# Retention heads worked between the units of the gate projection instead of after them

## The reference

```python
proj = h @ w_in                      # queries, keys: 4 heads x 256; values, gate: 4 heads x 512
...                                  # rotate q and k
o = fwd + bwd                        # per head: (q @ k.T * decay) @ v, in both directions
o = o * lax.rsqrt(jnp.mean(o * o, axis=-1, keepdims=True) + RMS_EPS)
return (jax.nn.silu(g) * o) @ w_out  # g: the gate, 2048 wide
```

## Time and profile before

| what | value |
|---|---|
| median of 3 runs | 2352.61 us (2351.33 to 2357.74) |
| the profiled execution, its own time | 2350.38 us |
| its span, first to last instruction | 2348.4 us |
| TensorE, VectorE, ScalarE busy | 98%, 72%, 57% of the span |
| mean granted TensorE clock | 0.999 of full |
| gate units and heads of layer 0 | about 102.4 to 167 us of the span |
| the same of layer 3 | about 1285 to 1349 us |

### The profile page before, as it was taken

The page is one execution under the profiler, slowest core; times in us unless marked ns, Lnnn a source line. Parts: engine busy times, 40 slices in busy tenths (PEclk is TensorE's granted clock), DMA queues, the critical chain, the costliest instruction groups (busy, mean ns, idle before and its releaser), DMA issues.

```text
span 2348.4 us, 55250 instructions
## 1 busy us (share of the span) xinstructions
PE 2309.2 (98%) x19883; PEld 2217.3 (94%) x19883; DVE 1689.1 (72%) x3317; ACT 1343.2 (57%) x2766; POOL 71.5 (3%) x140
## 2 busy tenths in 40 slices
PE   9999999999999999999999999999999999999998
PEld 8899999889998999999998999999898999998998
DVE  7667767977658888776576677658576785677875
ACT  5555556365556556665555565556755554466554
POOL 0000000000001112100000000000000000010000
PEclk9999999999999999999999999999999999999999
DMA  7535665235654455456645446654444555444664
GB/s 246 178 117 170 190 209 174 94 125 162 198 192 136 150 157 158 149 168 196 201 160 178 141 156 188 204 180 147 143 129 130 174 177 179 146 131 142 192 194 145
DMA packets 107520, 387.87 MB, mean 165 GB/s; under 512 B 14432, under 2 KB 16608, under 8 KB 107136
## 3 DMA queue, kind: packets, MB, share of 16 engines
q1 hardware_dynamic: 102656, 380.58, 51.2%
q0 software_dynamic: 4736, 5.58, 0.8%
HBM read 382.93 MB, written 1.05 MB: 164 GB/s over the span
## 4 chain that ended last, share of the span: by engine, by line
PE 83%; DVE 9%; ACT 4%; issue 2%; DMA 1%; POOL 0%; DVEq 0%; ACTq 0%; SPq 0%; POOLq 0%
PE acc L571 24%; PE acc L578 24%; PE acc L577 24%; DVE weights_lo L2178 2%; PE acc L791 1%; PE acc L790 1%; PE acc L789 1%; ACT weights_hi L1336 1%; PE acc L811 1%; DVE h L2337 1%; DVE y L2326 1%; DVE xn_parts L2333 1%; PE acc L724 1%; PE acc L894 1%; PE acc L916 1%
## 5 line engine op out<-in xcount | busy, mean ns | idle before, releaser
L2178 DVE TENSOR_TENSOR weights_lo<-weights,weights_hi 128x512 fp32r<-128x512 f32 (+1 forms) x1160 | 758.6, 680 | 323.6 <-ACT weights_hi L1336 318.9
L1336 ACT ACTIVATE weights_hi<-weights 128x512 fp32r<-128x512 f32 (+1 forms) x1160 | 679.8, 619 | 262.0 <-PE acc L578 233.2
L571 PE MATMUL acc<-xn_parts,weights_hi 128*128 128x256 f32 (+1 forms) x2560 | 726.9, 284 | 9.1 <-DVE weights_lo L2178 6.7
L578 PE MATMUL acc<-xn_parts,weights_lo 128*128 128x256 f32 (+1 forms) x2560 | 716.6, 280 | 0.0
L577 PE MATMUL acc<-xn_parts,weights_hi 128*128 128x256 f32 (+1 forms) x2558 | 716.0, 280 | 0.0
L571 PEld LDWEIGHTS acc<-xn_parts,weights_hi 128*128 128x128 f32 x2560 | 482.0, 188 | 22.9 <-issue 13.2
L571 PE MATMUL acc<-arena_r,weights_hi 128*128 128x256 f32 (+1 forms) x1760 | 494.2, 281 | 3.0 <-DVE weights_lo L2178 1.6
L578 PE MATMUL acc<-arena_r,weights_lo 128*128 128x256 f32 (+1 forms) x1760 | 490.9, 279 | 0.0
L577 PE MATMUL acc<-arena_r,weights_hi 128*128 128x256 f32 (+1 forms) x1754 | 488.8, 279 | 0.0
L578 PEld LDWEIGHTS acc<-xn_parts,weights_lo 128*128 128x128 f32 x2560 | 481.5, 188 | 0.0
L577 PEld LDWEIGHTS acc<-xn_parts,weights_hi 128*128 128x128 f32 x2558 | 481.1, 188 | 0.4
(11 more groups left out here) (341 smaller groups left out, 2302.4 us busy)
## 6 DMA issues: line engine op xcount, KB each, us to landing
weights<-in_ffn_in SPq DMA_DIRECT2D x176, 512.0 KB, 3.9
weights<-in_ffn_out SPq DMA_DIRECT2D x64, 704.0 KB, 4.1
weights<-in_att_in SPq DMA_DIRECT2D x72, 512.0 KB, 3.6
weights<-in_mlp_in SPq DMA_DIRECT2D x64, 512.0 KB, 3.6
weights<-in_mlp_out SPq DMA_DIRECT2D x64, 512.0 KB, 3.6
weights<-in_ret_qk SPq DMA_DIRECT2D x32, 512.0 KB, 4.0
weights<-in_ret_v SPq DMA_DIRECT2D x32, 512.0 KB, 3.9
weights<-in_ret_g SPq DMA_DIRECT2D x32, 512.0 KB, 3.5
```

What stands on the lines that cost most here:

```text
L571: nc.tensor.matmul(acc, hi, src_hi, start=first, stop=False)
L578: return nc.tensor.matmul(acc, lo, src_hi, start=False, stop=last)
L1336: nc.scalar.activation(w_hi[phase.ring(sub)][:, 0:n, :], raw[slot][:, j * SUB:j * SUB + n, :], ACT.Copy)\
L2178: nc.vector.tensor_tensor(w_lo[phase.ring(sub)][:, 0:n, :], raw[slot][:, j * SUB:j * SUB + n, :], w_hi[phase.ring(sub)][:, 0:n, :].bitcast ...
```

## The change

The two functions `ret_gates` and `retention` become one, `gates_and_heads`, on each of the three engines. The 16 gate units run as straight code, without a loop, and the steps of the heads stand between them: after gate unit 4h TensorE takes the mean of the squares of head h-1, weighs head h and computes the scores of head h+2; the other steps stand in fixed places on ScalarE and VectorE. All heads now use banks 6 and 7, so weighing head h waits until "gated" of head h-1 has read them. Banks 2 and 3 take the means, so the gate has two banks instead of four. Head 3 adds its squares on VectorE as the others do (three matmuls fewer). Since silu goes on between the heads, each inverse root is bracketed by two table loads, and the norm of the heads goes to a place of its own (`head_rstd`). After the last gate unit come the eight parts of the output projection. The lines of the kernel after lie some lines off those before.

```diff
+        head_rstd = silu[:, 0, 0:S1]
...
-            def retention(j, layer):
+            def gates_and_heads(j, layer, src):
...
-                def last_mean_square():
...
-                for hd in range(RET_HEADS):
-                    pe.wait_ge(R["p_ready"], 4 * j + hd + 1)
-                    if hd >= 2:
-                        pe.wait_ge(R["gated"], 4 * j + hd - 1)
-                    weigh(hd, 0)
...
+                def gate_unit(n):
+                    pe.wait_ge(out_evacuated, FREE_BANKS + gates.out0 + (n - 1 if n >= 2 else n - 3))
+                    multiply(gates, n // gates.body, n % gates.body, PS[:, n % 2, 0:S1], src, None, n == 3)
+
+                def weigh(hd):
+                    pe.wait_ge(R["p_ready"], 4 * j + hd + 1)
+                    if hd:
+                        pe.wait_ge(R["gated"], 5 * j + hd)
...
+                for n in range(gates.units):
+                    gate_unit(n)
+                    if n % 4 == 0:
+                        hd = n // 4
+                        if hd:
+                            mean_square(hd - 1)
+                        weigh(hd)
+                        if hd + 2 < RET_HEADS:
+                            ret_scores(j, hd + 2)
+                    if n == gates.units - 2:
+                        mean_square(RET_HEADS - 1)
                 part_output(0, 0, 0)
                 part_output(1, 0, 1)
-                last_mean_square()
                 part_output(2, 1, 0, True)
...
+                def inverse_rms(hd):
+                    exp_tables()
+                    act.wait_ge(R["sum_ready"], 4 * j + hd + 1)
+                    step(nc.scalar.activation(lnv[:, 0:S1], PS[:, 2 + hd % 2, 0:S1], ACT.Ln, bias=rms_eps, scale=float(D) / RET_V))
+                    nc.scalar.activation(head_rstd, lnv[:, 0:S1], ACT.Exp, scale=-0.5).then_inc(R["rstd_ready"], 1)
+                    nc.scalar.preload_act_table(ACT.Silu)
...
+                for n in range(gates.units):
+                    hd = n // 4
+                    if n + 1 < gates.units:
+                        split(gates, hd, n % 4 + 1)
+                    else:
+                        split(phase, 0, 0)
+                        inverse_rms(RET_HEADS - 1)
+                    if n % 4 == 1:
+                        if hd:
+                            inverse_rms(hd - 1)
+                        squares_of(hd)
+                    if n % 4 == 2 and hd:
                         rounded(hd - 1)
...
+                    gate(n)
+                split(phase, 0, 1)
+                split_part(phase, 0, 2, 0)
+                rounded(3, 0)
                 split_part(phase, 0, 2, 1)
+                rounded(3, 1)
+                exp_tables()
                 split_part(phase, 0, 3, 0)
...
+                for n in range(gates.units):
+                    hd = n // 4
+                    if n + 1 < gates.units:
+                        split(gates, hd, n % 4 + 1)
+                    else:
+                        split(phase, 0, 0)
+                        gated(3, 0)
+                    if n % 4 == 0 and hd:
+                        gated(hd - 1)
+                    if n % 4 == 1:
+                        if hd:
+                            scale(hd - 1)
                         added(hd)
...
+                    if n % 4 == 2:
+                        if hd:
+                            rest_of_head(hd - 1)
+                        if hd + 2 < RET_HEADS:
+                            decayed(j, hd + 2)
+                    gate(n)
+                split_part(phase, 0, 1, 0)
+                gated(3, 1)
+                split_part(phase, 0, 1, 1)
+                scale(3, 0)
...
```

More of the change, by code:

```diff
@@ L710, in ret_scores @@
                 last.then_inc(ret_sem["scores_ready"], 1)
-            def retention(j, layer):
+            def gates_and_heads(j, layer, src):
                 R = ret_sem
[L716 to L722, removed]
+                gates, phase = ph[f"ret_g{layer}"], ph[f"ret_out{layer}"]
+                def gate_unit(n):
[5 more added lines that the diff above has]
+                        pe.wait_ge(R["gated"], 5 * j + hd)
+                    for e in range(4):
+                        acc = PS[:, 6 + e // 2, (e % 2) * S1:(e % 2 + 1) * S1]
                         for kt in range(2):
@@ L725, in weigh @@
                                                     ret_p[:, hd % 2, kt * S1:(kt + 1) * S1], start=(kt == 0), stop=(kt == 1))
-                    if half:
-                        last.then_inc(R["o_ready"], 1)
+                    last.then_inc(R["o_ready"], 1)
                 def mean_square(hd):
-                    pe.wait_ge(R["squares_added"], 6 * j + 2 * hd + 2)
-                    nc.tensor.matmul(PS[:, hd % 2, 0:S1], mean, ret_sq[:, 0, :], start=True, stop=True).then_inc(R["sum_ready"], 1)
-                def last_mean_square():
[L735 to L738, removed]
+                    pe.wait_ge(R["squares_added"], 8 * j + 2 * hd + 2)
+                    nc.tensor.matmul(PS[:, 2 + hd % 2, 0:S1], mean, ret_sq[:, 0, :], start=True, stop=True).then_inc(R["sum_ready"], 1)
                 def part_output(sub, o, quarter, cut=False):
@@ L2656, in decayed, with gates_and_heads, gate, gated @@
                     .then_inc(ret_sem["p_ready"], 1)
-            def retention(j, layer):
+            def gates_and_heads(j, gates):
                 R = ret_sem
-                phase = ph[f"ret_out{layer}"]
+                phase = gates.after
                 first_split = 5 * j
-                def gated(hd):
-                    first = 6 if hd % 2 == 0 else 2
+                def gate(n):
+                    wait_unit(gates, n // gates.body, n % gates.body)
+                    dve.wait_ge(ret_gate_done, gates.units * j + n + 1)
+                    nc.vector.tensor_tensor(ffn_part[:, n % 4, :], PS[:, n % 2, 0:S1], rstd[:, 0:S1], ALU.mult)\
+                        .then_inc(ret_gate_scaled, 1)
+                    dve.wait_ge(ret_gate_scaled, gates.units * j + n + 1)
+                    dve.sem_inc(out_evacuated, 1)
+                def gated(hd, half=None):
+                    part = slice(0, 4) if half is None else slice(2 * half, 2 * half + 2)
                     dve.wait_ge(R["squares_ready"], 4 * j + hd + 1)
-                    g = proj1[:, 32 + 4 * hd:36 + 4 * hd, :]
-                    nc.vector.tensor_tensor(g, g, PS[:, first:first + 2, :].rearrange("p b (e t) -> p (b e) t", t=S1), ALU.mult)\
+                    dve.wait_ge(ret_gate_done, gates.units * j + 4 + 4 * hd + part.stop)
+                    g = proj1[:, 32 + 4 * hd:36 + 4 * hd, :][:, part, :]
+                    nc.vector.tensor_tensor(g, g, PS[:, 6:8, :].rearrange("p b (e t) -> p (b e) t", t=S1)[:, part, :], ALU.mult)\
                         .then_inc(R["gated"], 1)
@@ L2678, in scale @@
                     part = slice(0, 4) if half is None else slice(2 * half, 2 * half + 2)
-                    dve.wait_ge(R["gated"], 4 * j + hd + 1)
+                    dve.wait_ge(R["gated"], first_split + hd + (half or 0) + 1)
                     dve.wait_ge(R["rstd_ready"], 4 * j + hd + 1)
                     nc.vector.tensor_tensor(ret_o[:, part, :], proj1[:, 32 + 4 * hd:36 + 4 * hd, :][:, part, :],
-                                            spread(rstd[:, 0:S1], part.stop - part.start), ALU.mult).then_inc(R["scaled"], 1)
+                                            spread(head_rstd, part.stop - part.start), ALU.mult).then_inc(R["scaled"], 1)
                 def rest(hd, n):
```

76 lines of the change are left out of this document (15 added, 61 removed).

## The result

The changed kernel takes 2371.64 us (median of 4 runs, 2369.99 to 2374.42), the kernel before 2353.43 on the same chip (2351.33 to 2357.74): 18.2 us more, ratio 1.0077 with a 95% interval of 1.0064 to 1.0089. The forecast was 2369, slower, with a sum of 18.1.

A forecast was written before the change was run, and what follows sets the result against it. TensorE, busy 98% of the span, bounds the kernel. Stalls of 10.65 us plus restarts 0.9 less 2.5 saved make 9.1 a layer, 18.1 for two; added to the profiled 2350.4: 2368.5, forecast 2369, 8-in-10 range 2357 to 2376.

The forecast's parts named there:

- The chain of a gate unit: Scaling, silu, rounding and split on VectorE and ScalarE take 2.63 us against TensorE's 2.83 a unit: 0.2 to spare.
- "gated" before weighing: TensorE waits for VectorE's "gated" before weighing heads 1, 2 and 3: 1.0 us each, 3.0 a layer.
- Units 8, 11 and 12: TensorE waits for VectorE's lo halves at these gate units: 1.6, 0.45 and 1.35 us a layer.
- Output parts: TensorE waits at output projection parts 0, 2 and 6: 1.45, 2.2 and 0.6 us a layer.
- What goes: Two TensorE gaps (0.73 and 0.47) and three matmuls of head 3's mean (1.30) go: 2.5 us a layer.
- The loop that goes: The gate's loop, removed by the change, was said to cost little and was left out of the sum.
- Table loads at 1.30: Each ScalarE table load around a head's inverse root takes 1.30 us, its row in the profile, without a further drain.
- Rival (b): Part of the steps hides, tables costing nothing visible or some stalls overlapping: 2355 to 2362 us; 16%.
- Rival (c): ScalarE's table loads cost twice their row: 2391 us; 4%.
- Rival (a): The heads' steps hide between gate units, since by averages all fits; only 5.0 us go: 2345.4 us; 5%.
- Rival (d): The clock falls at the nine waits, a unit at 1.2 GHz taking 5.65 us: 2420 us; 2%.
- The two signs of an error: Wrong if units 6, 9, 10, 13, 14 were scaled within 0.3 us of their end, or TensorE's steps exceeded 0.118.

The follow-up runs named there:

- all moves: Changed kernel with "gated", "rest" and decay behind scalings, squares before the second table load, head 3's inverse root after the last silu, its last steps later: 2349.87 us.
- the straight gate: Kernel before with only the 16 gate units as straight code in two PSUM banks, heads after them as before: 2349.73 us, ratio 0.9984.
- the changed kernel with cuts: Changed kernel with one matmul of gate units 1, 5, 9 and 13 also cut in two halves, as unit 3 has it: 2373.51 us, ratio 1.0086.

## Why the prediction was right

- **The chain of a gate unit, 2.63 against 2.83.** Right: putting "rest" and the decay behind the scaling takes 9.8 us away without taking work away, and all moves together take 21.8, two table loads a layer among them.
- **"gated" before weighing, 3 x 1.0.** Right in place and releaser and nearly in size: 3.17 + 0.22 for the restarts, against 3.0 + 0.3.
- **Units 8, 11 and 12.** 3.88 + 0.23 against 3.4 + 0.3. Unit 8 waits 0.25 longer than supposed: VectorE has a further 0.18 of idle time before "rest", for ScalarE's rounding of the head (the row at 135.39).
- **Output parts.** 3.95 + 0.32 against 4.25 + 0.3: parts 0 and 2 were put 0.2 and 0.1 too late.
- **What goes, 2.5.** Right: neither the gap at the end of the gate, 0.73, nor that of 0.47 at the output is there after, and three matmuls a layer are gone.
- **The loop that goes, counted as nothing.** Wrong, by little: two turns cost 0.74 in layer 0 and 0.19 in layer 3. With it the terms give 11.77 - 2.51 - 0.74 = 8.5 in layer 0, against 8.6 measured; two small ones cancel (unit 15, which waits 0.1 and restarts, and 0.2 for the restarts behind the two old gaps).
- **The sum of 18.1 against 18.2.** In the two layers the sum is right to 0.5 us: 17.6 were measured. That the whole agrees to 0.1 is luck. The waits were put low, the loop was left out, and the granted clock is in no term: its mean is 0.9973 in the four executions of the changed kernel and 0.9989 in 45 later ones of the kernel before, which is, as an estimate, some 4 us of TensorE's time. What takes as much back elsewhere is not shown. The forecast of 2369 lies below the measured median mostly because the sum was added to the profiled execution, 2350.4, which lies below all four timed ones of its kernel; from their median of 2353.4 it is 2371.5.
- **Table loads at 1.30.** Right: 1.29 in succession. Rival (b) with free loads would be 2360; taking them out gave 2363.3. (In that sum the five stalls named fall by 4.15 and not by 3.9, and two restarts go with them and not three; 4.3 in all stays.) Rival (c), 2391, did not come.
- **Rival (a), the steps hide by averages.** False for this order, and true for another: with all moves they hide.
- **Rival (d), the clock falls at the waits.** Not at the nine waits of the profiled execution, where the clock is 1.00 in both windows above and in the same stretch of layer 3. But it does fall behind waits of this size in others, for less than the rival's price: 1.7 us at a time against 2.8.
- **The two signs of an error.** Units 6, 9, 10, 13 and 14 were scaled 2.3, 1.1, 2.6, 1.0 and 2.4 us after their ends, far over 0.3; the steps were 0.1134 or 0.1178, not longer than 0.118. ScalarE has nine table loads in layer 0 besides the first, as said.

## What to carry to other kernels

Where one engine is full and others feed it through a short ring, work moved in between costs what it adds to the chain that frees the next slot, however idle the engines are on average; put it behind the instruction that the chain waits for, not ahead of it. Before moving work, lay out that chain for one turn and ask how much later each step comes than the ring can cover. And measure the side changes of a move alone: here the straight code by itself gave as much as the straight code with the heads moved well.

## What the runs showed of the hardware

**Two steps.** The same fp32r matmul (128x128 by 128x256) goes at 0.1134 or 0.1178 us from start to start, and keeps one of the two for tens or hundreds of matmuls, until a wait, a plain float32 matmul or a cut comes in between. In the profiles before and after, some 10600 and 9860 steps were of the shorter kind and some 2100 and 2820 of the longer. None of the 177 cuts in eleven traces was followed by the longer one, where the kind could be told; what decides it otherwise stays open.

**Short falls of the clock.** The granted clock was 0.50 for 3.41 us at a time, behind some waits and not behind others of the same length. The same wait of TensorE in a later layer, whose code is the same in both kernels; first before, on the timeline:

```profile
1660.48 0.28 PE L578 MATMUL acc<-xn_parts,weights_lo 128*128 128x272 f32 x1
1662.69 0.37 PE L571 MATMUL acc<-xn_parts,weights_hi 128*128 128x272 f32 x1 [1.92 <-DVE weights_lo L2178]
```

and the window behind it, with the granted clock as the number after POOL:

```profile
1662.60:1668.00 5.40, 5.31 (x43) 5.34 (x44) 3.87 (x4) 5.40 (x11) 0.00 (x0) 1.00 0.45 121
```

Then after, on the timeline:

```profile
1679.59 0.28 PE L579 MATMUL acc<-xn_parts,weights_lo 128*128 128x272 f32 x1
1681.80 0.36 PE L572 MATMUL acc<-xn_parts,weights_hi 128*128 128x272 f32 x1 [1.92 <-DVE weights_lo L2184]
```

and the two windows of this profile in which the clock is low before its end:

```profile
1682.60:1685.80 3.20, 3.20 (x16) 3.20 (x15) 2.02 (x3) 3.18 (x6) 0.00 (x0) 0.50 0.55 164
2150.20:2153.40 3.20, 3.20 (x16) 3.20 (x15) 2.84 (x5) 1.26 (x3) 0.00 (x0) 0.50 0.30 120
```

Both waits are 2.21 from start to start; one is followed by 1.2 GHz, the other stays at 2.4. A stretch of 3.41 us at half clock does 1.7 us of full-clock work, so it costs TensorE 1.7, two of them 3.4. Outside the two stretches between the anchors the profile after also has 754 more of the longer steps, 3.3 us. These two are of the size of the 6.6 us by which the two executions differ there. That the change brings them about is not shown, and the first stretch speaks against it: it stands at the same wait in the kernel before with the straight gate (at 1661.5) and in the one with all moves (at 1661.2). In the changed kernel with cuts one such stretch falls into the heads, behind output part 2 on the timeline:

```profile
180.05 0.45 PE L572 MATMUL acc<-arena_r,weights_hi 128*128 128x256 f32 x1 [2.00 <-DVE weights_lo L2184]
```

and in the window:

```profile
180.30:183.50 3.20, 3.20 (x16) 3.20 (x16) 3.20 (x6) 1.62 (x4) 0.00 (x0) 0.50 0.30 61
```

So a wait of some 2 us can cost nearly twice its length, in one execution and not in the next. A single profile's difference of a few us should not be put down to a change before the clock of its windows has been read.
